# First attention: the scores of query blocks 0 and 1 of a head made in one go, three groups of score steps a head instead of four

## The reference, cut to what matters

```python
for i in range(S // Q_BLOCK):            # 4 query blocks of 128 tokens
    q0 = i * Q_BLOCK
    kend = q0 + Q_BLOCK
    qb, kb, vb = q[:, q0:kend], k[:, :kend], v[:, :kend]
    s = jnp.einsum('bqhcd,bkhcd->bhcqk', qb, kb)
    s = jnp.where(mask, s, -jnp.inf)
    p = jax.nn.softmax(s, axis=-1)
    w = p[:, :, 0] - lam * p[:, :, 1]
    outs.append(jnp.einsum('bhqk,bkhd->bqhd', w, vb))
```

## Time and profile before

| what | value |
|---|---|
| median of 3 runs | 1588.45 us |
| the profiled execution | 1588.53 us |
| its span, first to last instruction | 1586.7 us |
| PE busy | 1572.0 us (99%) |
| DVE busy | 917.7 us (58%) |
| ACT busy | 637.7 us (40%) |
| granted TensorE clock, mean | 0.998 of full speed |
| attention, first to last score step | 91.7 to 298.5 us |

### The profile page before, as it was taken

One profiled execution on the slowest core, in us unless ns is written; L12 is line 12 of the kernel. 1 busy time (PEld: TensorE's weight loads), 2 busy tenths in 40 slices (PEclk: granted clock), 3 DMA queues, 4 the chain that ended last, 5 costly groups with the idle time before them and its releaser, 6 DMA issues.

```text
span 1586.7 us, 19024 instructions
## 1 busy us (share of the span) xinstructions
PE 1572.0 (99%) x7374; PEld 1294.8 (82%) x7374; DVE 917.7 (58%) x1353; ACT 637.7 (40%) x994; POOL 81.8 (5%) x66
## 2 busy tenths in 40 slices
PE   9999999999999999999999999999999999999997
PEld 7877777878888888888887888888888888888886
DVE  7766887756644445357777545565655444434435
ACT  5445676643222222265444334344444322222212
POOL 3000000010000000040000010010002000000002
PEclk9999999999999999999999999999999999999999
DMA  5333232333333323233221242334133333332322
GB/s 202 113 101 101 79 92 76 100 126 94 99 101 93 106 93 94 93 93 96 81 67 60 74 133 87 113 121 145 53 93 96 109 99 97 94 105 94 96 84 74
DMA packets 49675, 155.64 MB, mean 98 GB/s; under 512 B 6193, under 2 KB 9137, under 8 KB 49457
## 3 DMA queue, kind: packets, MB, share of 16 engines
q1 hardware_dynamic: 49136, 153.85, 31.2%
q10 hardware_dynamic: 448, 0.57, 0.1%
HBM read 148.11 MB, written 2.10 MB: 95 GB/s over the span
## 4 chain that ended last, share of the span: by engine, by line
PE 95%; DVE 2%; DMA 1%; ACT 1%; issue 0%; SPq 0%; ACTq 0%; DVEq 0%
PE G L949 83%; PE SC L949 4%; PE TP L949 2%; PE O L949 2%; PE M L949 2%; PE TP L1298 1%; PE TP L1244 1%; DMA T<-QK 0%; DVE MGl L1848 0%; DVE X L2374 0%; DVE WL L1847 0%; DMA RAW<-in_va 0%; DMA QK<-T 0%; PE TP L1348 0%; ACT WH L1386 0%
## 5 line engine op out<-in xcount | busy, mean ns | idle before, releaser
L949 PE MATMUL G<-XGh,WH 128*128 128x512 f32 x1248 | 493.9, 396 | 0.0
L949 PE MATMUL G<-XGl,WH 128*128 128x512 f32 x1248 | 486.2, 390 | 0.0
L949 PE MATMUL G<-XGh,WL 128*128 128x512 f32 x1248 | 486.2, 390 | 0.0
L1847 DVE TENSOR_TENSOR WL<-RAW,WH 128x1024 fp32r<-128x1024 f32 (+3 forms) x281 | 339.1, 1207 | 181.6 <-ACT WH L1386 181.0
L1386 ACT ACTIVATE WH<-RAW 128x1024 fp32r<-128x1024 f32 (+3 forms) x281 | 283.8, 1011 | 184.2 <-PE G L949 173.1
L949 PEld LDWEIGHTS G<-XGh,WH 128*128 128x128 f32 x1248 | 234.4, 188 | 55.9 <-issue 5.6
L949 PEld LDWEIGHTS G<-XGh,WL 128*128 128x128 f32 x1248 | 234.3, 188 | 49.7
L949 PEld LDWEIGHTS G<-XGl,WH 128*128 128x128 f32 x1248 | 234.5, 188 | 46.7 <-issue 0.2
L949 PE MATMUL G<-MGh,WH 128*128 128x512 f32 x400 | 156.2, 391 | 0.9 <-ACT T L1725 0.6
L949 PE MATMUL G<-MGl,WH 128*128 128x512 f32 x400 | 155.8, 389 | 0.2 <-DVE MGl L1847 0.2
L949 PE MATMUL G<-MGh,WL 128*128 128x512 f32 x400 | 155.6, 389 | 0.0
(11 more groups left out here) (315 smaller groups left out, 1803.5 us busy)
## 6 DMA issues: line engine op xcount, KB each, us to landing
RAW<-in_up SPq DMA_DIRECT2D x32, 512.0 KB, 3.5
RAW<-in_dn SPq DMA_DIRECT2D x32, 512.0 KB, 3.5
RAW<-in_fg SPq DMA_DIRECT2D x22, 512.0 KB, 3.5
RAW<-in_fu SPq DMA_DIRECT2D x22, 512.0 KB, 3.5
RAW<-in_g SPq DMA_DIRECT2D x16, 512.0 KB, 3.7
RAW<-in_f SPq DMA_DIRECT2D x16, 512.0 KB, 3.5
X<-in_x SPq DMA_DIRECT2D x16, 256.0 KB, 4.1
RAW<-in_q SPq DMA_DIRECT2D x8, 512.0 KB, 3.7
```

Source lines behind the costliest of these rows:

```text
L949: return e.matmul(dst, st, mv, start=start, stop=stop, skip_group_check=True)
L1847: return e.tensor_tensor(dst, src, hi.bitcast(F32), ALU.subtract)
```

## The change

The steps of a head are planned in three groups (`GROUPS`): blocks 0 and 1 together, block 2, block 3, at `int(t * 7 / 3)` ticks, t = 3h + group: 0, 2, 4 in every head, still 7 ticks a head. Block 0's scores go to columns 256 to 383 of the bank (`columns_of`), block 1's to columns 0 to 255, so both fit in it beside each other, and the same in T, whose tiles now belong to a group (`group_of`, `last_of`). PE's second step of the group has no wait. DVE's passes over the group wait until all 12 matmuls of it are done, and the stages behind (`exp_a`, `weights_a`, `turn_a`, `wt_a`) of blocks 0 and 1 fall into one tick each. No matmul, DVE or ACT operation is added or taken away, and no table load of ACT (24 in both orders). The last group of a head comes at tick 4 in place of 5, and with it `pv_a` to `op_a`.

```diff
--- before.py
+++ after.py
@@ -55,13 +55,16 @@
            "a6 w3 b6 a7 b7")
 NAMES_A = {"q": "q", "k": "k", "a": "g0", "b": "g1", "u": "pool", "w": "wp"}
 HEADS_A = [(NAMES_A[word[0]], int(word[1])) for word in ORDER_A.split()]
-FIRST_A, WAIT_A, PACE_A, BACKLOG = 6, 2, 1.75, 6
+FIRST_A, WAIT_A, PACE_A, BACKLOG = 6, 2, 7 / 3, 6
 
 
 SPARE = -1
 
 
 FREED_BY = {2: 0, 3: 1, 4: 2, 5: 3, 7: 4}
+
+
+GROUPS = ((0, 1), (2,), (3,))
 
 
 
@@ -289,12 +292,13 @@
     def attention_a(self, start):
 
         done = {}
-        for s in range(32):
-            h, i = s // 4, s % 4
-            o = start + int(s * PACE_A) - self.clock
-            self.later(o, "scores_a", h, i)
-            for kind, n in STAGES_A:
-                self.later(o + n, kind, h, i)
+        for t in range(24):
+            h, group = t // 3, GROUPS[t % 3]
+            o = start + int(t * PACE_A) - self.clock
+            for i in group:
+                self.later(o, "scores_a", h, i)
+                for kind, n in STAGES_A:
+                    self.later(o + n, kind, h, i)
             if i == 3:
                 closing = CLOSING_A if h < 7 else CLOSING_LAST
                 for kind, n in closing:
@@ -696,9 +700,22 @@
 
             return 2 * (h % 4) + w
 
+        def group_of(s):
+
+            return 3 * (s // 4) + (0, 0, 1, 2)[s % 4]
+
+        def last_of(t):
+
+            return 4 * (t // 3) + (1, 2, 3)[t % 3]
+
+        def columns_of(i):
+
+            return slice(2 * P, 3 * P) if i == 0 else slice(0, (i + 1) * P)
+
         def weight_of(s, c):
 
-            return T[:, (3 + s % 3, 6 + s % 2)[c], 0:(s % 4 + 1) * P]
+            t = group_of(s)
+            return T[:, (3 + t % 3, 6 + t % 2)[c], columns_of(s % 4)]
 
         def w_tile(v):
 
@@ -1224,15 +1241,15 @@
                             q, k = ((QKh, QKh), (QKh, QKl), (QKl, QKh))[part]
                             if part == 0 and (h, i) == (0, 0):
                                 e.wait_ge(v_lo, VEV["vev", "va", 1, c])
-                            elif part == 0:
+                            elif part == 0 and i != 1:
                                 e.wait_ge(sa_max, 2 * SA[step] - 3 + c)
-                            t = mm(SC[:, c, 0:n], q[r, sq_, qs], k[r, sk_, 0:n], start=(part == 0), stop=(part == 2))
+                            t = mm(SC[:, c, columns_of(i)], q[r, sq_, qs], k[r, sk_, 0:n], start=(part == 0), stop=(part == 2))
                             if part == 2:
                                 t.then_inc(sa_done, 1)
 
                 elif kind == "turn_a":
                     h, i = arg
-                    src = T[:, 3 + (4 * h + i) % 3, :]
+                    src = weight_of(4 * h + i, 0)
                     if h == 0 and i < 2:
                         e.wait_ge(v_lo, VEV["vev", "va", 1, 2 + i])
                     else:
@@ -2091,14 +2108,15 @@
                         e.wait_ge(d_mask, 16)
                     if s >= 2:
                         e.wait_ge(sa_exp, 2 * (s - 1))
+                    g = group_of(s)
                     for c in range(2):
                         j = 2 * (s % 2) + c
-                        if c == 0 and s >= 3:
-                            e.wait_ge(turned, s - 2)
-                        if c == 1 and s >= 2:
-                            e.wait_ge(wa_done, s - 1)
-                        e.wait_ge(sa_done, 2 * s + c + 1)
-                        e.tensor_tensor_reduce(weight_of(s, c), SC[:, c, 0:n], MSK[:, S - n:S], -1.0, 3.0e38, ALU.add,
+                        if c == 0 and g >= 3:
+                            e.wait_ge(turned, last_of(g - 3) + 1)
+                        if c == 1 and g >= 2:
+                            e.wait_ge(wa_done, last_of(g - 2) + 1)
+                        e.wait_ge(sa_done, 2 * last_of(g) + c + 1)
+                        e.tensor_tensor_reduce(weight_of(s, c), SC[:, c, columns_of(i)], MSK[:, S - n:S], -1.0, 3.0e38, ALU.add,
                                                ALU.min, NM[:, j:j + 1]).then_inc(sa_max, 1)
 
                 elif kind == "weights_a":
```

## The result

The changed kernel takes 1584.70 us (median of 15 runs, 1583.80 to 1585.88); the kernel before, on the same chip at the same time, 1588.38 us (15 runs, 1586.57 to 1591.16). The ratio is 0.9979, with a 95% interval from 0.9972 to 0.9986: 3.3 us gained, between 2.2 and 4.4 (the two medians lie 3.7 apart). The profiled execution took 1583.8 us, its span is 1582.0 us.

What follows compares the result with a forecast made beforehand. PE, busy for 99% of the span, was taken to bound the kernel. The terms -2.8 + 0.15 - 1.4 - 0.33 = -4.4 us brought 1588.45 to 1584.1 us, range 1582.8 to 1586.9.

Steps and rivals of the forecast that it cites:

- One way in and out in place of two: PE's score matmuls of blocks 0 and 1: merged group costs 1.07 in place of 1.42 us, 2.8 us saved over 8 heads.
- Rival C: PE's score groups: 128-column pairs cost their columns alone, so merging saves 4.1 us; 1582.8 us, chance 0.08.
- Rival B: PE's merged score groups: the width change costs like a new group's first pair, saving less; 1584.9 to 1586.9 us, chance 0.13.
- The transposes: On PE, block 0's single transpose moves from behind `pv_a` to block 1's run in 7 heads: +0.15 us.
- The wait of `ss_a` of head 1: PE's wait for `sq_lo` from DVE at head 1's second sum goes: -1.4 us, with 1.0 us left over.
- Rival A: At head 1's `ss_a`: the reads of rotation 2 land late and the wait stays; 1585.5 us, chance 0.17.
- The end: At PE's low pass of k = 7, the wait for the last `sum_lo` goes: -0.33 us.
- What costs nothing, and its cover: Later DVE passes, moved weight splits and loads, POOL's operation and the bank's wait cost nothing; tightest weights have 4.0 us cover.
- rival D: `turn_a` of block 2 becomes PE's wait in every head; 1592.5 us if overshot by 1 us in 7 heads, chance 0.05.
- a small new wait: Somewhere unspecified, which no row names, a new wait of 1 to 2 us; chance 0.05.

Runs made afterwards that it cites:

- the wide block 0: The changed kernel with block 0's scores made for 256 keys in place of 128, the added ones masked and unread; 1585.38 us.
- the last version: The changed kernel with `sum_a` of head 5 ahead of the scores of (7, 3) on DVE, and head 0's first group one tick later; 1583.34 us.

## Why the prediction was right, and where not

The forecast was -4.4 us, to 1584.1; measured 1584.70, and a gain of 3.3 by the ratio. By its own steps:

- *One way in and out in place of two*: forecast -2.8 (a group of 1.07), found -2.7 (1.09), and shown by itself with the blocks apart (2.4 by the rows of seven heads, 2.05 in the medians). The pair price from the earlier trace rows, 0.11 us at 128 columns, was the right row to go by; 0.112 was found.
- *Rival C* is refuted, by the group's 1.09 and by the wide block 0, which cost 0.02 and not 0.16. The prediction quoted the Trainium skill, "TensorE: Matmul & The Clock Gate", section "Wait — 56ns, not 53.3ns?", with 55.6 ns at 128 columns. That figure is stated for matmuls back to back; here every matmul has a weight load of its own (7374 of each), and the trace doesn't agree: a narrow pair took 112 ns. At 256 columns the same rule would give an estimated 109 ns, and 118 were measured.
- *Rival B* is refuted as priced: the group cost 1.09, not 1.17 or more. But its mechanism is there, at half the price: the change of width costs 0.056 us, where B had 0.1. The forecast came out right beside it because a group that begins with narrow pairs has a first step shorter by 0.061 (0.163 in place of 0.224), which no term of the sum had. The two cancel, and that was luck. That the way in and out is paid once a visit is seen; why it costs what it does no run here shows. The Trainium skill, "TensorEngine Tiling (Array Packing)", section "Key Properties", says that a change of the tiling mode drains the engine. The longer step into a group (0.31 us in place of 0.23) would agree with that. The longer step out (0.34) says little, since it is also 0.32 behind transposes, which use all 128 rows.
- *The transposes*: forecast +0.15. Three ahead of block 3's scores cost 1.425 with them, two 1.317, and the single one behind `pv_a` had cost 0.09: 7 x 0.02 is +0.14. The choice near the first bound was right.
- *The wait of `ss_a` of head 1*: forecast -1.4, found: gone, 1.5 with the longer step behind it, and with 2.4 us of room where 1.0 was forecast. The reads of rotation 2 were there before DVE came to them; 1.3 of the room is that they landed sooner after their issue than in the kernel before (had they taken as long, rotation 2 would have begun at 160.3 and not at 158.95), which the prediction did not have. *Rival A* is refuted for these ticks. What the prediction didn't ask is whether a wait is worth its length. Here it was, because the ticks moved DVE's whole burst too: moved by itself, half of it came back one step further on.
- *The end*: forecast -0.33, found -0.34. The residual wait behind the split stayed, as said.
- *What costs nothing, and its cover*, is the step that failed. It put the moved weight splits at nothing because each comes two units ahead of its own use, and did not ask what stands behind a split on DVE. Likewise *rival D* said of the operations ahead of the first transpose's low half that "none of them waits for anything late"; around the end of head 6 the split did. I had followed DVE's queue for added operations, and weighed them against DVE's idle time, but not across to ACT: the passes over (7, 3) came ahead of `sum_a` of head 5, ACT's reading of the pool unit waits for that, ACT's WH stands behind it, and DVE's split and `sq_lo` behind that. The price was 0.82 us at `ss_a`, once and not in seven heads. *Rival D*'s wait, at `turn_a`, was not far: it lay hidden behind that of `ss_a`, and came out as 1.2 us when the sum was moved. (The rival's own figures had put 3.3 us of work on DVE against a room of 2.6, without saying how much of the 3.3 the 4.7 of the earlier trace rows already held.) The case of "a small new wait" was priced at 1 to 2 us; here it lay just under that, beside all the rest of the forecast.

The sum with these sizes: -2.7 + 0.14 - 1.5 - 0.34 + 0.82 = -3.6 (1.5 at head 1, with the longer step behind the wait), within the interval of both comparisons. The profiles differ by 4.7 in their spans; 0.9 of that is the first rotation's scatter, which the changed kernel's second profile did not have: its span is 3.5 below that of the kernel before. I had noted the 0.97 there as lying ahead of the change, and rightly left it out; that it varies by 2 us and more from run to run could not be seen in one profile.

What sets the floor of 0.11 us for a narrow pair stays open. The single transposes, with 128 columns of weights and 128 moving, also follow each other at 0.11, and so do the weight loads around a G (114.64 and 114.75), so that it may be the weight load and not the matmul; no run changed the weights alone. Open too are why the reads of rotation 2 land sooner in one order of ticks, whether the 0.75 by which the later `ss_a` of head 6 came out slower is all from the new wait (its rows give 0.4 more than the old one), what the extra tick of the last version is worth, and what scatters the DMAs of the first rotation.

## What to carry to other kernels

Small matmuls of another shape between long streams pay for the visit (0.34 to 0.40 us here) more than for their columns, so count visits first and columns second, and take the price from start-to-start distances, down to the single instruction where two effects could cancel. A wait on the bounding engine is worth its length only if the engine it waits for catches up behind it: before moving the waiting step, look at what the next steps ask of that engine (a wait can hide the next one), and rather move work on the late one. When an order shifts, follow each shifted operation to who waits for it on the other engines and back again, since an idle gap on the busy helper may be the far end of its own delay.

## What the runs showed of the hardware

- A pair of matmuls of 64 rows each, beside each other in the array, cost 0.112 us at 128 columns and 0.118 at 256, start to start inside a group: between these widths, columns were almost free. At 384 a group of three pairs cost 0.92 and at 512 1.10 (block 3 of head 0 in the last version, the only one without transposes ahead of it), 0.05 to 0.06 a pair more for each 128 columns, so there they count.
- The first pair of a group takes longer to the next start than those behind it, by its width: 0.163 at 128 columns, 0.224 at 256. Where the width changed from 128 to 256 inside the group, the first wide pair took 0.173 in place of 0.117.
- Of two profiles of one and the same kernel, one lost 0.15 and the other 1.0 us to the same four DMAs. One profile's DMA wait of this size is a sample and not a term.
- In the one profile where PE stood idle for 2.05 us at that wait, its granted clock was 0.50 (1.2 GHz) from 94 to 96 us, and the matmuls there lost another 1.0 us: a wait can cost more than its length.
